# A ring of three places for split weights, a second chunk in one pass over its tiles, and another order in the long convolutions

## The reference

```python
def first_block(x, p, ...):                  # two layers
    u = rms_norm(h, g);  proj = u @ w_in     # pool, conv, q, k, v and gates
    merged = g_a*(pooled @ w_pool_out) + g_b*(conv @ w_conv_out) + g_c*(diff_attn @ w_attn_out)
    h = h + merged @ w_o
    h = h + square(relu(rms_norm(h, g2) @ w_up)) @ w_down
    h = h + sigmoid(rms_norm(h, g3) @ w_ple_gate) * (p @ w_ple_proj)

def second_block(x, c, ctx, ...):            # layer 0: MLA and GQA attention; layer 1: hyena
    x = x + g1 * mixer(modulate(x, ...))
    x = x + g2 * square(relu(modulate(x, ...) @ w1)) @ w2

def hyena_mixer(h, ...):
    z = short_conv(h @ w_in, conv_w, conv_b);  x1, x2, v = split(z, 3)
    y = v
    for n, gate in enumerate((x1, x2)):      # two long convolutions over the sequence
        y = gate * (irfft(rfft(y) * K[n]) + y * skip[n])
    return y @ w_out
```

## Time and profile before

| | before |
|---|---|
| runs, us | 3493.21, 3497.33, 3483.47 (median 3493.21) |
| profiled execution, us | 3497.29, span in the trace 3495.3 |
| TensorE busy | 3312.2 us, 95% |
| VectorE busy | 2053.7 us, 59% |
| ScalarE busy | 1210.5 us |
| GpSimd busy | 643.5 us |
| mean granted TensorE clock | 0.972 of full speed |
| DMA | 342.95 MB, 98 GB/s over the span |

### The profile page before, as it was taken

The page is one execution under the profiler, slowest core; times in us unless marked ns, Lnnn a source line. Parts: engine busy times, 40 slices in busy tenths (PEclk is TensorE's granted clock), DMA queues, the critical chain, the costliest instruction groups (busy, mean ns, idle before and its releaser), DMA issues.

```text
span 3495.3 us, 36820 instructions
## 1 busy us (share of the span) xinstructions
PE 3312.2 (95%) x15132; PEld 2659.0 (76%) x15132; DVE 2053.7 (59%) x2663; ACT 1210.5 (35%) x1647; POOL 643.5 (18%) x495
## 2 busy tenths in 40 slices
PE   7999999999999999999988999989999888889998
PEld 5877777888787777888866776767778767777887
DVE  6655657664765565777557456564554567764443
ACT  3234442224433444222432333333343332333222
POOL 0000000000100003999610000003332023210000
PEclk9999999999999999999999899999999989899999
DMA  2222234542222223454311010022333221122222
GB/s 103 88 85 85 69 131 179 195 178 95 86 82 87 77 73 140 181 193 181 114 67 37 17 40 1 34 82 96 115 143 111 109 85 62 71 73 97 97 97 72
DMA packets 55623, 342.95 MB, mean 98 GB/s; under 512 B 5984, under 2 KB 7328, under 8 KB 18208
## 3 DMA queue, kind: packets, MB, share of 16 engines
q1 hardware_dynamic: 54080, 337.98, 26.9%
q10 hardware_dynamic: 1376, 2.62, 0.2%
HBM read 328.00 MB, written 12.58 MB: 97 GB/s over the span
## 4 chain that ended last, share of the span: by engine, by line
PE 71%; DVE 12%; POOL 10%; ACT 4%; issue 2%; DMA 0%; DVEq 0%; ACTq 0%; POOLq 0%
PE PS L262 69%; POOL FA L271 9%; DVE wl L271 2%; DVE FA L279 2%; PE PS L265 1%; DVE UL L271 1%; ACT wh L268 1%; DVE SC L279 1%; ACT SC L268 1%; DVE SC L288 1%; DVE SC L271 1%; ACT UH L268 1%; DVE FA L271 1%; DVE FA L288 1%; ACT FA L268 1%
## 5 line engine op out<-in xcount | busy, mean ns | idle before, releaser
L262 PE MATMUL PS<-UH,wh 128*128 128x512 f32 x2072 | 833.9, 402 | 42.6 <-DVE wl L271 21.6
L271 DVE TENSOR_TENSOR wl<-raw,wh 128x2048 fp32r<-128x2048 f32 (+2 forms) x255 | 560.3, 2197 | 446.1 <-ACT wh L268 446.0
L262 PE MATMUL PS<-UH,wl 128*128 128x512 f32 x2072 | 812.4, 392 | 0.0
L262 PE MATMUL PS<-UL,wh 128*128 128x512 f32 x2072 | 812.4, 392 | 0.0
L262 PE MATMUL PS<-RH,wh 128*128 128x512 f32 (+2 forms) x1688 | 672.4, 398 | 62.5 <-DVE UL L271 28.1
L262 PE MATMUL PS<-RL,wh 128*128 128x512 f32 (+2 forms) x1688 | 661.5, 392 | 0.0
L262 PE MATMUL PS<-RH,wl 128*128 128x512 f32 (+2 forms) x1688 | 661.3, 392 | 0.0
L268 ACT ACTIVATE wh<-raw 128x2048 fp32r<-128x2048 f32 (+2 forms) x255 | 454.6, 1783 | 320.1 <-PE PS L262 317.7
L262 PEld LDWEIGHTS PS<-UH,wh 128*128 128x128 f32 x2072 | 392.6, 189 | 160.0 <-issue 27.0
L262 PEld LDWEIGHTS PS<-UL,wh 128*128 128x128 f32 x2072 | 393.0, 190 | 84.4 <-issue 6.3
L262 PEld LDWEIGHTS PS<-UH,wl 128*128 128x128 f32 x2072 | 392.4, 189 | 83.6
(11 more groups left out here) (191 smaller groups left out, 3308.4 us busy)
## 6 DMA issues: line engine op xcount, KB each, us to landing
raw<-in_wall SPq DMA_DIRECT2D x224, 1024.0 KB, 4.8
FA<-in_wmod SPq DMA_DIRECT2D x48, 1024.0 KB, 4.8
raw<-in_wall SPq DMA_DIRECT2D x29, 512.0 KB, 3.5
kspec<-FA SPq DMA_DIRECT2D x8, 1024.0 KB, 7.5
FA<-kspec SPq DMA_DIRECT2D x8, 1024.0 KB, 4.8
PB<-in_window SPq DMA_DIRECT2D x16, 256.0 KB, 4.4
raw<-in_wall SPq DMA_DIRECT2D x8, 272.0 KB, 2.6
Hs<-in_xT ACTq DMA_DIRECT2D x4, 512.0 KB, 10.4
```

The lines of the kernel that those rows point to most:

```text
L262: return self.put(self.eng and self.eng.matmul(out, w, x, start=start, stop=stop, skip_group_check=True))
L271: return self.put(self.eng and self.eng.tensor_tensor(out, a, b, op))
```

## The change

- `wh` and `wl` get three places (`PLACES = 3`), `raw` keeps two. A call of `w_hi` or `w_lo` now splits up to the second piece after its tag (`ahead=2`), and no further than the next piece that isn't split (`blocked`). SBUF for the third place comes from a smaller scratch area for descriptors made in software (`dynamic_dma_scratch_size`); no DMA queue of this kernel uses that.
- The load of the transform matrices `cs` comes two and a half chunks later in the list.
- The second chunk behind a norm of `TWICE` takes tile by tile: six matmuls for each tile, three for either group. In the first block's layers the two head sums that stood behind its groups come after tiles 4 and 6.
- In the long convolutions TensorE does chunks 5, 7 and 9 in front of `signal(1)`, `(2)` and `(3)`. VectorE splits weights at the start of a chunk, in front of the short convolutions, does `products_low` between the chunk's two groups, and splits the signal behind chunks 5, 7 and 9. ScalarE does its `products` between the two groups as well, and the scaling by `skip` after the next butterfly.

The diff, cut to its core (the order of steps goes on in the same way for s = 2 and 3):

```diff
 RAWS = 2
+PLACES = 3
...
             for j in range(4):
                 load(("up", M, q, j), ("sum", ("up", M, q, 2 * j + 1)), piece(up, l, 0, 8, 1024 * q + 256 * j, 256))
-                if M == 2 and q == 0 and j == 1:
-                    load(("cs",), ("sum", ("sv", 3, 1, 3)), *[piece(n, None, 0, 4, 0, 256) for n in ("C", "S")], split="own")
             for j in range(4):
                 load(("dn", M, q, j), ("sum", ("dn", M, q, 2 * j + 1)), piece(down, l, 1024 * q, 8, 256 * j, 256))
+                if M == 2 and q == 0 and j == 0:
+                    load(("cs",), ("sum", ("sv", 3, 1, 3)), *[piece(n, None, 0, 4, 0, 256) for n in ("C", "S")], split="own")
 
...
-        raw=sb("raw", [128, RAWS * RAWN]), wh=sb("wh", [128, RAWS * RAWN], FR),
-        wl=sb("wl", [128, RAWS * RAWN], FR),
+        raw=sb("raw", [128, RAWS * RAWN]), wh=sb("wh", [128, PLACES * RAWN], FR),
+        wl=sb("wl", [128, PLACES * RAWN], FR),
...
-        a = (place[i] % RAWS) * RAWN + o
+        a = (place[i] % PLACES) * RAWN + o
...
+        def from_x(tag, keys, frees, n, of=range(8), by_tile=False, between=None):
             p.wait_ge("w_lo", tag)
+            if by_tile:
+                for key, fr in zip(keys, frees):
+                    take(key, *fr, of=of)
+                for k in range(8):
+                    for e in x_made(n, k):
+                        p.wait_ge(*e)
+                    for m, key in enumerate(keys):
+                        three(ps(key), pair(tag, 256 * k + 128 * m), X(n, k), k == 0, k == 7)
+                        if k == 7:
+                            p.then_inc("sum", key)
+                    if between is not None:
+                        between(k)
+                return
             for m, key in enumerate(keys):
                 take(key, *frees[m], of=of)
...
+                    tag, keys = ("up", M, q, j), [("up", M, q, k) for k in ks]
+                    frees = [[("r_x" if M < 2 or first else "r_sq", (M, q, k))] for k in ks]
+                    if first:
+                        first_x(tag, keys, frees, n)
+                    else:
+                        from_x(tag, keys, frees, n, by_tile=n in TWICE and q == 0 and j == 1)
...
+                if i == 1:
+                    from_x(("qk", l, 1), [("qk", l, k) for k in ks], [[("qk_x", (l, k))] for k in ks], n, by_tile=True,
+                           between=lambda t: head_sum(l, t // 2 - 2) if t in (4, 6) else None)
+                    continue
...
-                    if i == 1 and m == 0:
-                        head_sum(l, 0)
+                    if i == 2 and m == 0:
+                        head_sum(l, 2)
...
-                    from_x(tag, keys, [[("hw", (j, m))] for m in range(2)], 8, of=low)
+                    from_x(tag, keys, [[("hw", (j, m))] for m in range(2)], 8, of=low, by_tile=j == 1)
...
             spectra(0, 1)
             inverse(0, 0)
+            chunk(5)
             signal(1)
-            chunk(5)
             spectra(1, 0)
...
+        def blocked(tag):
+
+            return any(plan[x][4] is False for x in range(index[tag] + 1, halves_of[done[0]] - 1))
+
+        def w_hi(tag, ahead=2):
+
+            while done[0] < len(halves_of) and before(halves_of[done[0]]) <= place[index[tag]] + ahead and not blocked(tag):
...
-                elif place[i] >= RAWS:
-                    a.wait_ge(*plan[ring[place[i] - RAWS]][5])
+                elif place[i] >= PLACES:
+                    a.wait_ge(*plan[ring[place[i] - PLACES]][5])
...
-            def chunk(j):
+            def chunk(j, between=None):
...
+                tile(j, 0)
+                if between is not None:
+                    products(*between)
+                tile(j, 1)
+
+            def tile(j, m):
...
+            def skip(s):
+                od, hf = STEPS[s]
+                a.wait_ge("sum", ("sg", s, 3))
                 for i in range(4):
                     k = 4 * hf + i
                     a.activation(fat(VV, k), fat(VV, k), ACT.Copy, scale=col("h_skip_2", 0, 8 * od + k)).then_inc("xs", (s, i))
...
-            chunk(0)
-            chunk(1)
-            chunk(2)
+            for j in range(3):
+                chunk(j)
             signal(0)
             chunk(3)
             butterfly(0, 0)
-            chunk(4)
-            products(0, 0)
+            skip(0)
+            chunk(4, (0, 0))
             butterfly(0, 1)
+            chunk(5, (0, 1))
             signal(1)
-            chunk(5)
-            products(0, 1)
             butterfly(1, 0)
-            chunk(6)
-            products(1, 0)
+            skip(1)
+            chunk(6, (1, 0))
             butterfly(1, 1)
...
-            def chunk(j):
+            def chunk(j, between=None):
                 w_lo(("hw", j))
                 for m in range(2):
+                    if m and between is not None:
+                        products_low(*between)
                     k = 2 * ((j + 8) % 12) + m
                     x, y = book.place["hw", j, m] if book.counted else 0, conv_tile(k)
...
-                if j < 11:
-                    w_lo(("hw", j + 1))
...
             products(0, 0)
-            chunk(4)
-            products_low(0, 0)
+            chunk(4, (0, 0))
             products(0, 1)
+            chunk(5, (0, 1))
             signal(1)
-            chunk(5)
-            products_low(0, 1)
             products(1, 0)
-            chunk(6)
-            products_low(1, 0)
+            chunk(6, (1, 0))
             products(1, 1)
...
-    nc = _bacc.Bacc("TRN2", target_bir_lowering=False, num_devices=1)
+    nc = _bacc.Bacc("TRN2", target_bir_lowering=False, num_devices=1, dynamic_dma_scratch_size=1024)
```

More of the change, by code:

```diff
@@ L552, in group @@
             p.then_inc("sum", key)
-        def from_x(tag, keys, frees, n, of=range(8)):
+        def from_x(tag, keys, frees, n, of=range(8), by_tile=False, between=None):
             p.wait_ge("w_lo", tag)
+            if by_tile:
[11 more added lines that the diff above has]
+                return
             for m, key in enumerate(keys):
@@ L1126, in hyena @@
             inverse(1, 0)
+            chunk(7)
             signal(2)
-            chunk(7)
             spectra(2, 0)
@@ L1133, in hyena @@
             inverse(2, 0)
+            chunk(9)
             signal(3)
-            chunk(9)
             spectra(3, 0)
@@ L1168, in scalar_program @@
         two = Turns([0, 1])
-        def w_hi(tag, ahead=1):
-            while done[0] < len(halves_of) and before(halves_of[done[0]]) <= place[index[tag]] + ahead:
+        def blocked(tag):
+            return any(plan[x][4] is False for x in range(index[tag] + 1, halves_of[done[0]] - 1))
+        def w_hi(tag, ahead=2):
+            while done[0] < len(halves_of) and before(halves_of[done[0]]) <= place[index[tag]] + ahead and not blocked(tag):
                 i = halves_of[done[0]]
@@ L1665, in chunk @@
                         a.wait_ge("k_out%d" % f, 3)
[L1666 to L1684 removed]
+                tile(j, 0)
[3 more added lines that the diff above has]
+            def tile(j, m):
+                key, k = ("hw", j, m), 2 * ((j + 8) % 12) + m
+                s = conv.take(a, ("hw_y", k))
+                book.place[key] = s
+                if 8 <= k < 16:
+                    a.wait_ge("vx_g", ((k - 8) // 4, k % 4))
+                middle = dict(bias=col("h_conv_b_2", 0, k), scale=col("h_conv_w_2", 0, 24 + k))
+                if j:
+                    a.wait_ge("sum", key)
+                    a.activation(sc(s, 8, 520), ps(key), ACT.Copy)
+                    a.activation(conv_tile(k), ps(key), ACT.Identity, **middle).then_inc("hw", (j, m))
+                else:
+                    a.wait_ge("hw_x", (0, m))
+                    a.wait_ge("ws", 8)
+                    a.activation(sc(s, 8, 520), sc(s, 8, 520), ACT.Identity, bias=ST[:, 5, m:m + 1])
+                    a.settle()
+                    a.activation(conv_tile(k), sc(s, 8, 520), ACT.Identity, **middle).then_inc("hw", (0, m))
             def signal(s):
[L1687 removed]
                 for t4 in range(4):
@@ L1791, in vector_program, with blocked, w_lo @@
         pairs = Turns([2, 3])
-        def w_lo(tag, ahead=1):
-            while done[0] < len(halves_of) and before(halves_of[done[0]]) <= place[index[tag]] + ahead:
+        def blocked(tag):
+            return any(plan[x][4] is False for x in range(index[tag] + 1, halves_of[done[0]] - 1))
+        def w_lo(tag, ahead=2):
+            while done[0] < len(halves_of) and before(halves_of[done[0]]) <= place[index[tag]] + ahead and not blocked(tag):
                 i = halves_of[done[0]]
```

48 lines of the change are left out of this document (10 added, 38 removed).

## The result

The changed kernel took 3467.76 us (median of 6 runs, 3459.57 to 3472.92), the kernel before 3491.76 us (3483.47 to 3501.66) beside it: ratio 0.9923, 95% interval 0.9903 to 0.9944. It is 24 us faster. I had forecast 3440 us, with 3425 to 3455 us as that forecast's own range and 3412 to 3470 us as the range of 8 in 10. The direction was right and the time lies in the wide range, at its slow end; the gain is less than half of the forecast's 53 us.

The account below looks back on a forecast made before the run. TensorE's work was taken to bound the kernel, leaving its 183 us of idling and the lower clock to gain. Terms summed to -54.8 us, from 3497.3 to 3442.5 profiled, 3440 as median; 8-in-10 range 3412 to 3470.

Parts of the forecast that it names:

- A: Long convolutions up to `spectra(1,0)`: chunk 3 starts 9.7 us earlier and the way on is 10.3 us shorter, -20.0 us.
- rival 3: The lead doesn't come because loads wait for splits; A loses 8 us, D and E 2.7 each; some 3452 us; chance 0.09.
- B: Two periods of the long convolutions, 66.0 and 67.5 us: each becomes 54.5 us with a 4.8 us wait, -24.5 us.
- Rival 1: VectorE binds the convolutions, so A and B are halved to -9 and -13.5; some 3460 us; chance 0.17.
- C: From `spectra(3,0)` to the end of the convolutions: the pair of small waits goes twice, -5.6 us.
- D: Norm 9: fewer matmuls after the last tile by tile, and the 2.70 us wait for `wl` goes, -7.5 us.
- E: Norm 7: same sum as D gives -7.6 us, halved for the filters' network to -3.7, range 0 to -7.6.
- F: Norms 0 and 3, by tile: little to be had, -1.5 us, with ends of -15 and +4.2.
- G: End of layer 1's MLP: ScalarE's earlier splits wait for late loads and delay the tiles' streams, +8 us, between 0 and 10.
- H: All other splits, with 24.0 us of waits for `wl`: a longer lead is used up once, 0, ends -24 and +5.
- rival 2: The waits for `wl` go as well and the clock stays up: H gives -12 to -24, some 3420 us; chance 0.10.
- Rival 4: First block's MLPs: ScalarE waits for SP's queued loads, TensorE loses up to 1.9 us per chunk; 3533 us; chance 0.04.

Follow-up runs that it names:

- e4: Changed kernel with a lead of one piece everywhere; orders, by-tile passes and third place stay: 3484.33 us, ratio 0.9969 to the kernel before.
- e9: e1 with the signal's split directly after chunks 5, 7 and 9, products' low parts and weight split behind it, ScalarE's high parts after the signal's copy: 3422.95 us.
- e10: e5 with the second chunk behind norms 7, 8 and 9 by group again, lead of two kept: 3443.81 us, ratio 0.9848.
- e8: e1 with the long convolutions in the old order on all three engines, keeping three places, lead of two and by-tile chunks: 3472.96 us, ratio 0.9930.
- e2: Changed kernel with both layers' second qk chunk by group and a lead of one at layer 1's last two MLP pieces: 3449.12 us, ratio 0.9867.
- e1: Changed kernel with a lead of one for all first-block splits and its second qk chunks by group, second block as changed: 3442.09 us, ratio 0.9850.
- e3: Changed kernel with a lead of one at the first qk piece, ao and wo pieces and first-quarter up pieces in the first block: 3463.00 us, ratio 0.9910.
- e5: e1 with VectorE's weight split in chunks 5, 7 and 9 moved behind the signal's split: 3436.43 us, ratio 0.9822.

## Why the prediction was right or wrong

**A, right.** -18.0 against -20.0. The first signal's chain through the load of `hw` 4 was the one that I had followed. ScalarE and VectorE in it:

```profile
2806.06 1.91 ACT L269 ACTIVATE wh<-raw 128x2048 fp32r<-128x2048 f32 x1 [3.83 <-DMA raw<-in_wall]
```

```profile
2808.00 2.29 DVE L272 TENSOR_TENSOR wl<-raw,wh 128x2048 fp32r<-128x2048 f32 x1 [1.57 <-ACT wh L269]
```

From the end of the split of `hw` 3 at 2801.3 to chunk 3 at 2813.9 it took 12.6 us, where the terms of the prediction add up to 12.7. But the lead was worth only 3.3 us in A (e4), where rival 3 had 8.

**B, mechanism right, size not.** -15.9 against -24.5. "It waits 4.8 us instead of 7.28" failed: it was 7.26. The working took VectorE's operations at the durations which they had beside an idle GpSimd (2.2 for the split, 1.5 for the convolutions) and put them where GpSimd adds the products. That cost 3.0 us per signal, of which a product's split at 0.68 us gave 1.1 back; and the products began 2.0 us behind the point from which the 13.0 us of chunk and transposes count, not 1.1. The trace before could have warned: at 2894.50 a pair of convolutions took 3.48 us. "The pairs of 1.78 and 1.06 go" failed for one of two pairs, and 0.88 us in front of chunk 7 were not foreseen. In sum a period has 9.8 us of waits where I had 4.8; its clock cost 1.8 us against the busy 47.4 us of e9, where I had 3.1. Rival 1 (VectorE binds) is what happened in B, -15.9 against its -13.5, but not in A, where it took off 11 us for one signal. The rule on the shared ports which I weighed for a gain of 6.6 us applies with the other sign: VectorE's busy time in a period rose from 47.3 to 51.7 us, and GpSimd's from 24.0 to 28.8: the new order made them meet more often. The Trainium skill ("SBUF — State Buffer", "SBUF: two separate sides") says that either of the two can be the one that waits. The rows of 3.39, 3.41 and 3.32 us agree.

**C and D, right in size.** -5.6 and -8.5 against -5.6 and -7.5. In D the pass needs the lead: alone it brings 1.1 us and then loses it. The lead doesn't need the pass: alone it brings 4.4 us, more than its addend of 2.70 (e4, e10). C I had put down to the order alone; the waits that it was to take away are gone, but with the lead of one the stretch gives only 1.1 us (e4), with the old order and the lead nothing (e8). It took both.

**E, low.** -6.3 against -3.7. I had halved the sum for ScalarE's chain of the filters; a wait of 4.40 us for it did appear, at 2362.46, but less than half of the 7.6 us was lost. Without the lead nothing is left (e4), without the pass 4.7 us (e10).

**F, wrong.** -1.5 against +15.7, the largest miss. The step was "little is to be had", with +4.2 as its worst end. Without the 2.5 us in front of the norm it is still 13.2. I had asked only what the tiles cost TensorE and not who reads the chunk's two groups. The pass brings the first group later by half a chunk, and VectorE, which binds the four qk chunks, reads it at once. e2 shows it: by group nothing is lost, with the lead of two and its double split still there.

**G, right in place.** +11.3 against +8; e2 takes it away.

**H, wrong by 9 us.** "A lead is used up once and doesn't return" holds, but a split one piece earlier also stands in front of work that it delays: 4.83 and 4.24 us in place of 3.20 and 1.48. e1 and e3 show it. So rival 2 was half true: of the 24.0 us for `wl` only the 6.7 us at the program's start are left, and nothing was gained.

**Rival 4, its cause without its price.** ScalarE now waits for loads in front of its splits, 196.8 us in sum where it was 2.4, and SP's waits for VectorE's modulation rose from 354.9 us (longest 10.7) to 475.1 (longest 30.5), so that sign, SP's waits shorter, failed there. But TensorE loses only 0.4 and 0.9 us in the two MLPs from behind their first chunks. Of the other signs, the waits behind norm 9 and at the sums of squares came as told, the periods of 54 to 55 us didn't, and the summed waits for `UL` stayed below 40 us.

**The range.** That 3467.76 us lies within 3412 to 3470 is in good part luck. The range reached that far for rival 1, VectorE in the convolutions, and that is the smaller miss: B fell short by 8.6 us, the first block by 29.6, which no rival had. The unexplained 5.9 us of the second attention made up for a part.

The second attention gave -5.9 us with no cause in the change. Kernels with the same instructions up to its end differ in it by as much (e1 -3.3, e8 -13.2, e9 -0.6), and so do the first 55 us of the program (e1 -1.9, e5 +3.9). Between those kernels it is the clock and not the waits: in the second attention TensorE waits 33.6, 33.7 and 32.2 us in e1, e8 and e9, and is busy for 524, 514 and 528 us at a granted clock of 0.96, 0.97 and 0.95; in the first 55 us it is busy for 29.5 us in e1 and 35.3 in e5. What makes the clock differ stays open, and so does the part of the -5.9 us that is shorter waits (28.9 us against 32.6). Single traces are read no finer than that in these two stretches.

## What to carry to other kernels

Before a split or a pass is moved forward, ask what stands behind it in its engine's list and who reads each result first, group by group: an earlier transfer or a later first result costs most where another engine binds. A wait in front of a busy engine is the rest of a whole list, so take an instruction with slack out of that list (here the products' low parts, which had 5.45 us), and don't trust that the releaser which the trace names is the one that binds. An earlier consumer pays only if what it consumes is earlier too: the pass by tile brought nothing without the lead, the lead something without the pass.

## What the runs showed of the hardware

Where VectorE's and GpSimd's two-input operations on SBUF met, one took its free time only once the other had ended: a split of 2.29 us took 3.39, a pair of convolutions of 1.54 took 3.41 to 3.48, one GpSimd addition of 1.28 took 3.32. And a wait cost more than itself: periods with a longest wait of 3.47 to 5.14 us ran at a mean granted clock of 0.90 to 0.95, those with waits up to 1.76 us at 1.00. By TensorE's busy time that was 1.8 us in the changed kernel's first period and 3.9 in e5's, with the shorter wait in e5: how much comes on top isn't told by the length of the wait.
